# Reordering the copies, splits and low parts around the first attention and feed-forward of a two-block transformer kernel

## What is computed

```python
for l in range(2):
    sh1, sc1, g1, sh2, sc2, g2 = split(silu(c) @ w_ada[l] + b_ada[l], 6)
    h = x * (1 + sc1) + sh1
    y = mixer_ab(h) if l == 0 else mixer_cd(h)      # attention heads, then @ w_o
    x = layer_norm(ALPHA * x + (1 + g1) * y)
    h = x * (1 + sc2) + sh2
    g, u = split(h @ w_in, 2);  y = (silu(g) * u) @ w_out
    x = layer_norm(ALPHA * x + (1 + g2) * y)
```

## Time and profile before

| | us |
|---|---|
| median of 3 runs | 1261.98 |
| lowest and highest | 1260.16, 1263.48 |
| the profiled execution | 1264.81 |
| its span, first to last instruction | 1263.0 |

### The profile page before, as it was taken

One profiled execution on the slowest core, in us unless ns is written; L12 is line 12 of the kernel. 1 busy time (PEld: TensorE's weight loads), 2 busy tenths in 40 slices (PEclk: granted clock), 3 DMA queues, 4 the chain that ended last, 5 costly groups with the idle time before them and its releaser, 6 DMA issues.

```text
span 1263.0 us, 16569 instructions
## 1 busy us (share of the span) xinstructions
PE 1207.7 (96%) x6603; PEld 834.0 (66%) x6603; DVE 665.2 (53%) x1185; ACT 506.3 (40%) x761; POOL 51.1 (4%) x96
## 2 busy tenths in 40 slices
PE   6998899999899999999999999999999999999987
PEld 2697578788789977887877787445444544544446
DVE  5588868687769786664468476111111111111126
ACT  1478553443465676343445375111112111111126
POOL 0100000000000000101001200000000000000000
PEclk9999999999999999999999999999999999999999
DMA  9998859888746555867556769999999999999990
GB/s 370 390 332 221 332 191 300 314 317 312 285 181 218 201 179 197 311 213 204 200 192 221 252 252 404 426 426 427 426 427 425 426 422 427 424 426 426 424 388 34
DMA packets 50811, 396.03 MB, mean 314 GB/s; under 512 B 7265, under 2 KB 9505, under 8 KB 12226
## 3 DMA queue, kind: packets, MB, share of 16 engines
q1 hardware_dynamic: 38466, 337.17, 67.7%
q0 software_dynamic: 9072, 54.97, 12.5%
q10 hardware_dynamic: 3216, 3.10, 1.0%
HBM read 391.73 MB, written 3.49 MB: 313 GB/s over the span
## 4 chain that ended last, share of the span: by engine, by line
PE 74%; DMA 11%; DVE 9%; ACT 3%; issue 1%; SPq 1%; DVEq 0%; POOL 0%; ACTq 0%
PE psum L1315 16%; PE psum L748 8%; PE psum L751 8%; PE psum L755 8%; PE psum L1359 8%; PE psum L1243 4%; DMA slabs<-in_w 3%; DMA w_raw<-in_units 2%; PE psum L1251 2%; PE psum L803 2%; DMA staged<-in_ada 2%; PE psum L807 2%; PE psum L805 2%; DVE w_parts L2048 2%; DMA gate_rows<-drv 2%; DVE aring L2031 2%
## 5 line engine op out<-in xcount | busy, mean ns | idle before, releaser
L2048 DVE TENSOR_TENSOR w_parts<-w_raw,w_parts 128x2048 fp32r<-128x2048 f32 x106 | 242.1, 2288 | 90.2 <-ACT w_parts L1449 90.1
L1449 ACT ACTIVATE w_parts<-w_raw 128x2048 fp32r<-128x2048 f32 x106 | 202.1, 1912 | 100.7 <-DMA w_raw<-in_units 100.5
L1315 PE MATMUL psum<-slabs,arena 128*64 128x512 f32 x896 | 223.1, 592 | 2.7 <-issue 2.5
L748 PE MATMUL psum<-w_parts,h_parts 128*128 128x512 f32 x416 | 166.2, 400 | 5.1 <-DVE act_tm L2237 3.6
L751 PE MATMUL psum<-w_parts,h_parts 128*128 128x512 f32 x416 | 163.3, 393 | 0.0
L1315 PEld LDWEIGHTS psum<-slabs,arena 128*64 128x64 f32 x896 | 74.3, 137 | 110.8 <-issue 108.6
L1449 ACT ACTIVATE arena<-psum 128x512 f32<-128x512 f32 (+1 forms) x59 | 33.3, 568 | 270.8 <-PE psum L1329 140.8
L755 PE MATMUL psum<-w_parts,h_parts 128*128 128x512 f32 x416 | 111.6, 390 | 0.0
L2031 DVE CUSTOM_DVE_ANT_0 aring<-aring,cb 128x1024 f32<-128x1024 f32 x80 | 94.5, 1219 | 4.8 <-DMA aring<-in_ada 4.7
L748 PEld LDWEIGHTS psum<-w_parts,h_parts 128*128 128x128 f32 x416 | 78.6, 189 | 24.2 <-DVE act_tm L2237 5.3
L755 PEld LDWEIGHTS psum<-w_parts,h_parts 128*128 128x128 f32 x416 | 78.3, 188 | 16.8
(11 more groups left out here) (325 smaller groups left out, 1792.5 us busy)
## 6 DMA issues: line engine op xcount, KB each, us to landing
w_raw<-in_units SPq DMA_DIRECT2D x110, 1024.0 KB, 5.7
slabs<-in_w SPq DMA_DIRECT2D x30, 2048.0 KB, 18.6
slabs<-in_w SPq DMA_DIRECT2D x52, 1024.0 KB, 16.8
aring<-in_ada POOLq DMA_DIRECT2D x40, 1024.0 KB, 6.9
arena<-in_w SPq DMA_DIRECT2D x16, 2048.0 KB, 19.6
w_odd<-in_w SPq DMA_DIRECT2D x16, 2048.0 KB, 21.6
w_odd<-in_w SPq DMA_DIRECT2D x16, 1024.0 KB, 19.9
staged<-in_ada SPq DMA_DIRECT2D x8, 1024.0 KB, 16.1
```

The source lines that it names most:

```text
L748: mm(psum[:, bank, :], high(tile, tok), w_hi(k)[:, col:col + 512], start=first and bank not in begun, stop=False, skip_group_check=True)
L1315: ins = nc.tensor.matmul(psum[s * CAP:(s + 1) * CAP, w, :], xe_t[:, kt, s * CAP:(s + 1) * CAP], up_weights(w, s, b, kt), start=kt == 0, st ...
L1449: return nc.scalar.activation(out_ap, in_ap, func, **kw)
L2048: v.tensor_tensor(w_lo(k), raw(k), w_hi(k).bitcast(F32), ALU.subtract).then_inc(w_split, 1)
```

## The change

Five moves, none of which adds or removes an instruction.

1. ACT, step j = 7 of the query/key units, both layers: the copy `take_qk` goes ahead of `beat`, that is of the head squares (first layer) or pair 3's high part (second layer) and of the exponentials of pair 5.
2. ACT, first layer: `first_gate_back` goes from ahead of pair 5's high part to behind the probabilities of pair 6.
3. DVE, both layers: `pair_low` of pair 7 goes ahead of one piece (18 in the first layer, 43 in the second).
4. DVE, both layers: the split of unit `FF_AT` goes from ahead of the norm's first sums to behind `derive`.
5. ACT and DVE, both layers: the high and the low half of feed-forward group 0 go ahead of the split of unit `FF_AT + 5`.

```diff
@@ -1674,9 +1674,12 @@
                 for j in range(8):
+                    if j == 7:
+                        take_qk(layer, j)
                     if j >= 2:
                         beat(layer, j - 2)
-                    take_qk(layer, j)
+                    if j < 7:
+                        take_qk(layer, j)
                     if j >= 3:
                         for i in items_of(layer, j - 3):
                             take_probs(layer, i)
@@ -1702,13 +1705,13 @@
                 split(u + WO_AT + 3)
-                if layer == 0:
-                    first_gate_back()
                 take_pair(layer, 5)
                 exps(layer, 14)
                 exps(layer, 15)
                 take_probs(layer, item[12])
                 take_probs(layer, item[13])
+                if layer == 0:
+                    first_gate_back()
                 take_pair(layer, 6)
@@ -1730,8 +1733,8 @@
                 gate(layer, 0, 1)
+                act_highs(layer, 0)
                 split(u + FF_AT + 5)
-                act_highs(layer, 0)
                 gate(layer, 1, 1)
@@ -2357,9 +2360,8 @@
                 if layer == 0:
                     piece(17)
+                pair_low(layer, 7)
                 piece((18, 43)[layer])
-                pair_low(layer, 7)
-                split(u + FF_AT)
 
                 q = 2 * layer
                 ln_residual(q, 0)
@@ -2368,6 +2370,7 @@
                 if layer == 0:
                     piece(19)
                 derive(2 * layer)
+                split(u + FF_AT)
                 split(u + FF_AT + 1)
                 ln_second(q)
@@ -2378,8 +2381,8 @@
                 gated_up(layer, 0, 1)
+                act_lows(layer, 0)
                 split(u + FF_AT + 5)
-                act_lows(layer, 0)
                 gated_up(layer, 1, 1)
```

## The result

The changed kernel took 1269.98 us (median of 9 runs, 1266.2 to 1275.8), the kernel before 1261.98 (9 runs, 1258.0 to 1267.09). The ratio is 1.0069, with an interval of [1.0053, 1.0086]: 8.7 us slower, between 6.7 and 10.9. The forecast was 1269.8. The profiled execution took 1271.59 us, with a span of 1269.8 at a mean clock of 0.989; before it was 1263.0 at 0.991. Of the 6.8 us between the spans, 2.6 are clock (1269.8 x 0.011 = 14.0 against 1263.0 x 0.009 = 11.4, each uncertain by some 0.6, since the clock has three digits), and 4.2 are waits; clock that is lost while PE waits anyway counts as clock in this split. Busy times hardly moved (before: the earlier trace rows).

A forecast was written before the change was run, and what follows sets the result against it. TensorE, busy 96% of the span, was taken as the bound. First layer 0.6 + 1.0, second 1.8 + 1.0, make +4.4 us; with 3.4 of half clock +7.8, so 1269.8 us against the median 1261.98; range 1264.5 to 1272.5.

The forecast's parts named there:

- part 1: Query/key copy: first-layer gap moves to the low products, gain 0 (bounds 0 and +0.9 us); second layer +0.45 us.
- part 2: First layer, gate's way back issued later: ScalarE's 1.45 us wait goes, gain 1.5 us up to near 131.
- part 3: Last low part earlier: first-layer 2.23 us gap closes but gains 0, token rows hold the norm; second layer +0.3 us.
- first sum: First layer's norm: its first sum follows the token rows' landing, at 138.2 instead of 139.69, after 4 us idle.
- part 4: Split moved behind the norm's sums: net first layer, the first four moves, +0.6 us; second layer 2.2 us of delay.
- part 5: Feed-forward halves ahead of splits: product for the first down projection comes later, +1.0 us in each layer, gaps 2.4 us.
- second layer, second norm: Transposes of 477.23: 2.95 us of delay less 1.18 us of idle time used up, +1.8 us.
- cold stretches behind three gaps: Half clock behind growing gaps at 477, 179 and 497 us: 1.7 us each, two of three taken, 3.4 us.
- later loads at half rate: First layer, earlier unit loads halving the token rows' rate for the last 2 us: landing near 139, an estimate.
- Rival (d): First layer's norm follows PE and VectorE, not the token rows: faster, 1261.1 us where no stretch turns cold; chance 0.08.
- Rival (c): Feed-forward halves do nothing, PE waits for the low half: 1264.4 to 1266.1 us; chance 0.09.
- rival (a): The clock does not fall behind the grown gaps, or falls once: 1266.4 to 1268.1 us; chance 0.27.

The follow-up runs named there:

- part 1 alone: Kernel before with only the last query/key copy moved ahead of head squares or high part and exponentials, both layers: ratio 1.0011, interval 0.9997 to 1.0025.
- part 3 alone: Kernel before with only the last pair's low part put ahead of one piece, both layers: ratio 1.0024, 3.0 us slower.
- rows early: Kernel before with the token rows' load issued ahead of the unit load that waits for TensorE: ratio 1.0011.
- part 5 alone: Kernel before with only the high and low feed-forward halves put ahead of the splits, both layers: ratio 1.0025, 3.2 us slower.
- ScalarE's half: Kernel before with only the high feed-forward half ahead of ScalarE's split, VectorE's order kept: ratio 1.0069 against the kernel before.
- the change with rows early: Changed kernel with the token rows' load issued ahead of the unit load: ratio 1.0045 against the kernel before, 3.0 us less than the change.

## Why the prediction held

**Its sum was right, and most of its terms; that the median came within 0.2 us of it is luck.** What each step said, and what the trace of the changed kernel shows:

| step | said | shown |
|---|---|---|
| part 1, low products, gap | 110.8, 2.9 | 110.88, 2.68 |
| part 1, copy of heads | 114.3 | 114.77 |
| part 2, sixth pair's high part | 121.6 | 122.01 |
| part 3, gap at last low product | none | none |
| first sum | 138.2 | 139.37 |
| idle before it | 4 | 4.89 |
| part 4, low part of normed rows | 150.9 | 152.06 |
| part 4, second norm's transposes | 158.3 | 159.45 |
| part 5, gaps | 2.4, 2.4 | 2.42, 2.46 |
| part 4, second layer's low part | 471.6 | 473.19 - 1.6 = 471.6 |
| second layer, second norm | +1.8 | 3.4 - 1.6 = +1.8 |
| cold stretches behind three gaps | two | one |

**Part 1** was taken at 0 in the first layer and cost 0.5: its own bound, 0 to 0.9, named the way (half clock ahead of the transposes), and the choice of 0 because copy and split touch was wrong by that much; part 1 alone shows ScalarE as the one that waits. In the second layer ScalarE's high part is 3.5 us late as said (439.11 less 1.6 of delay so far is 437.5).

**Part 2** was mis-sized, and this is the term that failed. ScalarE's side came as worked out, less the 0.5 us of part 1. The rows' landing was put at 138.2 and came at 139.3: the load was issued 1.1 us earlier, not 1.5, and took 8.9 us from issue, not 8.1. Everything behind follows: low part and second norm are each 1.15 us later than said, with no other error. The trace of before had no case of a slower landing, and carrying its 8.1 us as a constant was the slip. The alternative that the text gave, later loads at half rate, put it near 139, which is the right time for the wrong reason: in part 3 alone a unit load follows on the same queue 1.8 us before the landing, and the landing stays at 8.1 us. The Trainium skill (DMA: Bandwidth & Descriptors, Queues, rings and completion order) says that on each DMA engine the descriptors are consumed in ring order; that run agrees.

**Part 3** was right in both layers as the change has it: nothing in the first, since the rows hold the norm. The rows early on the kernel before and on the changed one are the direct evidence. The second layer's norm began 2.4 - 1.6 = 0.8 us late, with 0.75 worked out for parts 1 and 3. That 0.3 us for part 3 holds only beside part 4. Rival (d), the norm following PE, is refuted by the profile of the changed kernel, where the wait carries the rows' name.

**Part 4** was right in mechanism and size: 2.2 us ahead of the low part in each layer, 1.2 of it absorbed in the second. Alone it costs 3.8 us, but in the first layer only; in the second the cost needs part 3 beside it.

**Part 5** was right: gaps of 2.4 us, by way of ScalarE's split. Rival (c), that it does nothing, falls with part 5 alone (1.0025, all of the interval above 1).

**The clock.** Two cold stretches of three were forecast and one came in the profiled execution; by its clock it was rival (a)'s case, for which 1268.1 stood. The waits came to 2.2 us at the first down projection, 1.8 more at the second layer's second norm and 1.0 more at its down projection: 5.0 us for 4.4 worked out. The difference is the late landing's 1.15, of which 0.5 was gone again at the transposes of the first feed-forward group (175.64 against 174.40, 1.2 us late). The cold stretch at 501 us added 1.4, and the one near 347 us, which of the two kernels only the one before had, took off 0.6. That makes 5.8 us behind 504 us, where 7.8 had been worked out. From there the delay did not simply reach the end: 1.1 us was won back near 587, where PE had waited 0.79 us before and waits no more, and 2.2 us were lost behind 760, with no edit near. So the +6.8 of this execution meets the +7.8 partly by luck.

All runs together say more on the clock than one trace. Span x (1 - granted clock) is 14.2 us on average over the nine runs of the changed kernel (standard error 1.2), and 9.2 to 9.4 over the 29 to 34 runs of the kernel before on each of three chips. That is 4.9 us more, near three stretches of 1.7. Outside the clock the changed kernel has 1254.5 us and the kernel before 1250.2 to 1252.2: 2.3 to 4.4 us more. So the total held, with about as much clock as waits in it, where 3.4 and 4.4 had been worked out. Some of that clock is lost under waits, as at 142.6 to 145.5, and where a usual run has its stretches is not shown. What the runs show is that there is no fixed number: the gap of 2.4 to 3.1 us at the first down projections fell cold in both layers of part 5 alone and of ScalarE's half, in one of two layers in the changed kernel and in the change with rows early, and the gap of 2.46 us before the first projection, cold before, was followed by full clock in ScalarE's half of part 5. Eleven traces have that gap, 2.45 to 2.47 us long: in five half clock follows, in six it does not. In this window of ScalarE's half a PE that had stood for 2.46 us goes on at 1.00:

```profile
108.00:110.00 2.00, 1.24 (x6) 1.05 (x7) 1.93 (x6) 1.98 (x6) 0.00 (x0) 1.00 1.01 410
```

So the price of such a gap is a chance of 1.7 us, and two of three was no better founded than one or three. The range had room for that.

**Left open.** Why part 2 slows the rows' load; how often each gap falls cold, beyond these counts; what the clock does behind 588 us; and what part of the 0.0011 of part 1 is real.

## What to carry to other kernels

Before an operation is moved out of a place, look whether the time there was free: in the first layer the split of part 4 lay under a wait for a load, and moving it behind the work that the load releases cost its whole length. Before a gap of the busiest engine is closed, name the last arrival at the next meeting point; closing 2.2 us of gap ahead of a norm that waited for its rows moved them into that norm's gap. Name the one behind it too: with the rows there in time, the sum won 2.3 us of the 4.9 it had waited, and then waited for GpSimd's piece. And where two engines split the same unit in turn, anything put ahead of the first engine's share delays the second's, and all that is queued behind it.

## What the runs showed of the hardware

- The same load of 1 MB of token rows took 8.0 or 8.1 us from issue to landing in seven kernels, 8.9 and 10.9 in the two that have part 2 and the load in the same place; its issue on SP took 0.43 us in the seven and 0.92 to 0.95 in the two.
- A small transfer on ScalarE's queue, issued under a 1 MB load on SP's, landed after 12.5 to 14.0 us in four traces; without that load it took 11.0 to 11.7 in seven.
- Idle gaps of 2.4 to 3.1 us of TensorE are followed by half clock in some executions and not in others, at the same place of the program: the 2.46 us gap before the first projection in five traces of eleven.
